# First attention layer of a four-layer stack on one core: the projection as pairs of half-row chunks, with its groups moved into the last pair and the output projection

## The reference

```python
def swa_sink_attention(h, w_qkv, q_gain, k_gain, sinks, w_o):
    qkv = h @ w_qkv                         # 1024 -> 1024 (q) + 256 (k) + 256 (v)
    q = rmsnorm(q, q_gain); k = rmsnorm(k, k_gain)   # per head of 64
    # 4 key/value heads, 4 query heads for each; a query sees the last 128 keys
    scores = q @ k / 8 - slope * dist, masked
    p = softmax([scores, sink])[..., :-1]
    return (p @ v) @ w_o                    # 1024 -> 1024
```

## Time and profile before

| | us |
|---|---|
| median of 3 runs | 1301.46 |
| lowest, highest | 1301.07, 1302.06 |
| span of the profiled execution (first to last instruction) | 1299.9 |
| TensorE matmul busy in it | 1265.0 (97%) |
| VectorE, ScalarE, GpSimd busy | 900.1, 697.7, 139.2 |
| chain that ended last: TensorE, VectorE, ScalarE | 81%, 11%, 4% |

### The profile page before, as it was taken

The page is one execution under the profiler, slowest core; times in us unless marked ns, Lnnn a source line. Parts: engine busy times, 40 slices in busy tenths (PEclk is TensorE's granted clock), DMA queues, the critical chain, the costliest instruction groups (busy, mean ns, idle before and its releaser), DMA issues.

```text
span 1299.9 us, 19368 instructions
## 1 busy us (share of the span) xinstructions
PE 1265.0 (97%) x7906; PEld 1125.9 (87%) x7906; DVE 900.1 (69%) x1151; ACT 697.7 (54%) x894; POOL 139.2 (11%) x168
## 2 busy tenths in 40 slices
PE   9999999999899999999999999999999999899997
PEld 8888888889688888889888888889999999888886
DVE  6876655667866666567877666588898885865556
ACT  5445555456655455444844444448876763444441
POOL 0000000005604000010000000000325342000000
PEclk9999999999799999999999999999999999999999
DMA  8675766644158766666146555554544335465551
GB/s 276 200 232 159 215 194 194 195 162 163 34 146 211 215 187 188 190 182 213 42 163 226 189 188 189 186 168 151 154 139 142 127 117 169 162 208 188 189 193 64
DMA packets 214888, 224.52 MB, mean 173 GB/s; under 512 B 7312, under 2 KB 192016, under 8 KB 214672
## 3 DMA queue, kind: packets, MB, share of 16 engines
q1 hardware_dynamic: 211472, 213.41, 51.5%
q10 hardware_dynamic: 2304, 7.77, 1.7%
q0 software_dynamic: 1024, 2.10, 1.0%
HBM read 222.20 MB, written 1.05 MB: 172 GB/s over the span
## 4 chain that ended last, share of the span: by engine, by line
PE 81%; DVE 11%; ACT 4%; issue 2%; POOL 2%; DMA 1%; DVEq 0%; SPq 0%; ACTq 0%
PE ps L509 20%; PE ps L733 19%; PE ps L500 12%; PE ps L520 7%; PE ps L530 5%; DVE wlo L1607 3%; PE ps L1028 3%; PE ps L694 2%; ACT whi L1143 2%; PE ps L481 2%; PE ps L483 2%; PE ps L482 2%; PE ps L492 1%; DVE ssm_taps L2055 1%; PE ps L599 1%
## 5 line engine op out<-in xcount | busy, mean ns | idle before, releaser
L1607 DVE TENSOR_TENSOR wlo<-raw,whi 128x2048 fp32r<-128x2048 f32 x202 | 462.9, 2300 | 143.2 <-ACT whi L1143 142.5
L1143 ACT ACTIVATE whi<-raw 128x2048 fp32r<-128x2048 f32 x202 | 384.4, 1908 | 58.3 <-PE ps L733 29.7
L509 PE MATMUL ps<-act,whi 128*128 128x512 f32 x1264 | 300.3, 390 | 0.0
L509 PEld LDWEIGHTS ps<-act,whi 128*128 128x128 f32 x1264 | 235.0, 188 | 47.2
L500 PEld LDWEIGHTS ps<-act,wlo 128*128 128x128 f32 x1416 | 181.0, 191 | 8.0 <-DVE wlo L1607 1.8
L500 PE MATMUL ps<-act,wlo 128*128 128x256 f32 x1416 | 184.0, 283 | 1.2 <-DVE wlo L1607 1.2
L1190 ACT ACTIVATE low_sb<-ps 128x512 f32<-128x512 f32 x88 | 52.4, 595 | 186.4 <-PE ps L500 186.4
L520 PE MATMUL ps<-whi,act 128*128 128x256 f32 x736 | 136.0, 285 | 1.3 <-DVE act L1688 1.3
L520 PEld LDWEIGHTS ps<-whi,act 128*128 128x128 f32 x736 | 115.2, 191 | 2.7 <-DVE act L1688 1.3
L733 PE MATMUL ps<-whi,hidhi 128*128 128x512 f32 x368 | 114.1, 391 | 1.2 <-DVE hidlo L1812 1.2
L733 PE MATMUL ps<-wlo,hidhi 128*128 128x512 f32 x368 | 113.7, 390 | 0.0
(11 more groups left out here) (236 smaller groups left out, 1748.0 us busy)
## 6 DMA issues: line engine op xcount, KB each, us to landing
raw<-in_mlp_w SPq DMA_DIRECT2D x128, 512.0 KB, 4.4
raw<-in_ffn_w_gate_up SPq DMA_DIRECT2D x88, 512.0 KB, 5.2
raw<-in_ssm_w_in SPq DMA_DIRECT2D x50, 512.0 KB, 4.8
raw<-in_ffn_w_down SPq DMA_DIRECT2D x44, 512.0 KB, 5.0
raw<-in_conv_w_in SPq DMA_DIRECT2D x24, 512.0 KB, 4.7
raw<-in_attn_w_in SPq DMA_DIRECT2D x18, 512.0 KB, 4.8
raw<-in_ssm_w_out SPq DMA_DIRECT2D x16, 512.0 KB, 4.1
raw<-in_attn_w_qkv SPq DMA_DIRECT2D x12, 512.0 KB, 4.4
```

Of the source, the lines that this page charges most:

```text
L509: e.matmul(bank2(b + f), hi[:, k, f * P:(f + 1) * P], act[:, :, k, :], start=k == 0, stop=False, skip_group_check=True)
L1143: e.activation(whi[s][:, :], raw[s][:, :], ACT.Copy).then_inc(*rounded.up(c))
L1607: e.tensor_tensor(wlo[s][:, :], raw[s][:, :], f32(whi[s][:, :]), ALU.subtract).then_inc(*split.up(c))
```

## The change

The projection is cut into three pairs of `half_rows` chunks of 512 columns: keys and values, queries 0 to 511, queries 512 to 1023. Each pair gives one bank for each token tile, with 512-wide matmuls. Copies, squares, sums, rates, norms and transposes now go by pair `p` and token tile `m`. Groups are ordered `m = n // 2 % 2, g = 2 * (n // 4) + n % 2`: groups 0 and 1 are the first token tile, 2 and 3 the second, with the first eight heads; 4 to 7 the same with the last eight. All groups use one pair of score banks (2 and 3) and one bank for `mix` (6), so `score(n)` waits for `biased(n - 1)` and `mix(n)` for `out_lo(n - 1)`. Groups 0 to 3 stand between the products of the last pair. Groups 4 to 7 stand between those of the output projection, whose chunks now come as upper rows of both column halves, then lower rows. The four output tiles end in banks 0, 1, 7 and 2. VectorE adds `x` only in `next_stage`, after `lo(FFN1)`. A second factor of 1.0 stands in `make_bias`.

The diff, cut to its core:

```diff
         def swa_group(n):
-            m, g = divmod(n, 4)
+            m, g = n // 2 % 2, 2 * (n // 4) + n % 2
...
+        PAIR_COLS = (D, 0, 512)
+        PAIR_BANKS = ((0, 1), (2, 3), (0, 1))
+        PROJECTED = {(0, 0): 0, (1, 0): 1, (0, 1): 7, (1, 1): 2}
...
-            for n in range(QKV1 // WIDE):
-                columns(SWA + n, A["attn_w_qkv"][0], QKV_COLS["swa"][n])
-            for n in range(4):
-                half_rows(SWA + 6 + n, A["attn_w_o"][0], n)
+            for p in range(3):
+                for half in range(2):
+                    half_rows(swa_pair(p, half), A["attn_w_qkv"][0], half, PAIR_COLS[p])
+            for half in range(2):
+                for col in range(2):
+                    half_rows(swa_out(half, col), A["attn_w_o"][0], half, 512 * col)
...
# TensorE, swa()
+                take(0)
+                e.wait_ge(*split(swa_pair(0, 0)))
+                e.wait_ge(*act_lo(2, 0, 0))
+                rows(0, 0, 0)
+                e.wait_ge(*rounded(swa_pair(0, 1)))
+                e.wait_ge(*act_lo(2, 0, 1))
+                for j in range(2):
+                    rows(0, 1, 0, (2 * j, 2 * j + 1), (0, 2))
+                    turn_tile(2, 1, (j,))
+                e.wait_ge(*split(swa_pair(0, 1)))
+                rows(0, 1, 0, passes=(1,)).then_inc(*tile_made.up("swa", 0, 0))
...
+                e.wait_ge(*split(swa_pair(2, 0)))
+                rows(2, 0, 0, (0, 1))
+                heads(1, 0, 6)
+                rows(2, 0, 0, (2, 3))
+                score("swa", 0)
+                e.wait_ge(*split(swa_pair(2, 1)))
+                rows(2, 1, 0).then_inc(*tile_made.up("swa", 2, 0))
+                heads(1, 1, 7)
+                score("swa", 1)
+                e.wait_ge(*copied("swa", 0, 1))
+                rows(2, 0, 1, (0, 1))
+                turn_probs("swa", 0)
+                score("swa", 2)
+                rows(2, 0, 1, (2, 3)).then_inc(*multiplied.up(swa_pair(2, 0)))
+                mix("swa", 0)
+                turn_probs("swa", 1)
+                score("swa", 3)
+                rows(2, 1, 1, (0, 1))
+                mix("swa", 1)
+                heads(2, 0, 7)
+                turn_probs("swa", 2)
+                score("swa", 4)
+                rows(2, 1, 1, (2, 3)).then_inc(*multiplied.up(swa_pair(2, 1)))
+                mix("swa", 2)
+                turn_probs("swa", 3)
+                score("swa", 5)
...
+                out_rows(0, 0, 0)
+                mix("swa", 3)
+                e.wait_ge(*qk_lo("swa", 2, 0))
+                heads(2, 1, 7)
+                turn_probs("swa", 4)
+                score("swa", 6)
...
+                out_rows(1, 0, 0).then_inc(*part.up("swa", 0, 0))
+                mix("swa", 7)
+                e.wait_ge(*split(swa_out(1, 1)))
+                out_rows(1, 1, 0).then_inc(*part.up("swa", 0, 1))
+                e.wait_ge(*out_lo("swa", 6))
+                out_rows(1, 0, 1, (0, 1))
+                e.wait_ge(*out_lo("swa", 7))
+                out_rows(1, 0, 1, (2, 3)).then_inc(*multiplied.up(swa_out(1, 0)))
+                for k in range(4):
+                    last = out_rows(1, 1, 1, (k,))
+                    if k in (1, 2):
+                        turn_tile(3, 0, (k - 1,))
+                last.then_inc(*multiplied.up(swa_out(1, 1)))
                 free.clear()
-                project("swa", SWA + 6, 3, lambda p: out_lo("swa", 4 + p), True)
+                free[0], free[1], free[2] = added("swa", 0, 0), added("swa", 1, 0), added("swa", 1, 1)
...
# ScalarE, swa()
+                exps(2)
+                mix(0)
+                turn(1)
+                hi(swa_out(0, 0))
+                heads(2, 0, 7)
+                exps(3)
+                mix(1)
+                turn(2)
+                copy(2, 1)
+                square_heads(2, 1)
+                exps(4)
...
+                turn(7)
+                mix(7)
                 e.wait_ge(*biased("swa", N_GROUPS - 1))
                 load_rows(3, A["norm_ffn"][1])
-                project("swa", c0 + 6, 3)
+                hi(FFN1)
+                next_stage(3, "swa", FFN1 + 1, (0, 1))
...
# VectorE, swa()
+                weigh(1)
+                heads(1, 1, 7)
+                normalise(0)
+                head_sum(2, 0)
+                weigh(2)
+                normalise(1)
+                rest(0)
+                head_norm(2, 0)
+                weigh(3)
+                normalise(2)
+                rest(1)
+                heads(2, 0, 7)
+                lo(swa_out(0, 0))
+                weigh(4)
+                head_sum(2, 1)
+                normalise(3)
...
+                lo(FFN1)
+                next_stage(3, FFN1 + 1, sum_tile)
...
# GpSimd
             make_bias(0)
-            head_rate(0)
+            head_rate(0, 0)
+            head_rate(0, 1)
             make_bias(1)
-            for n in range(1, 5):
-                head_rate(n)
-            for n in range(2, N_GROUPS):
+            head_rate(1, 0)
+            head_rate(1, 1)
+            make_bias(2)
+            head_rate(2, 0)
+            make_bias(3)
+            make_bias(4)
+            head_rate(2, 1)
+            for n in range(5, N_GROUPS):
                 make_bias(n)
```

440 lines of the change are left out of this document (260 added, 180 removed).

## The result

| | before | changed |
|---|---|---|
| median of 4 runs each, us | 1301.76 | 1313.44 |
| lowest, highest | 1301.07, 1302.40 | 1312.94, 1314.31 |
| ratio, 95% interval | 1 | 1.0091 [1.0079, 1.0102] |
| span of the profiled execution | 1299.9 | 1311.3 |
| TensorE, VectorE, ScalarE, GpSimd busy | 1265.0, 900.1, 697.7, 139.2 | 1267.7, 899.6, 697.7, 128.8 |

The forecast was 1309.7 us within 1302.3 to 1315.8: the sign and the range held, and the time came out 3.7 us above the number. The loss lies in the touched layer: the changed trace is 0.25 us late ahead of it (its first product starts at 290.85 instead of 290.60), and the first transpose of token tile 1 for the next FFN stands at 400.27 instead of 389.33, +10.9 us of the span's +11.4. That transpose marks the end of the layer in what follows.

A forecast was written before the change was run, and what follows sets the result against it. TensorE, busy 97% of the span, was taken as the bound. Terms 3.1 + 1.6 - 1.8 + 0.5 + 2.0 + 2.0 + 0.9 = +8.3 us raised the span to 1308.2, hence a median of 1309.7 us, range 1302.3 to 1315.8.

The forecast's parts named there:

- Wait at the start, +3.1: Layer start: TensorE runs out of products and waits 3.8 us for VectorE's low part of chunk 50, costing 3.1 us.
- Half clock behind it, +1.6: After the wait at the layer's start, TensorE runs at half clock and loses 1.6 us, ends 0 and 1.9.
- Wide matmuls, -1.8: Projection: 144 matmuls of 512 columns replace 288 of 256, taking 32.8 us instead of 34.6, a gain of 1.8 us.
- The groups' waits, +0.5: Attention groups: TensorE's waits for VectorE plus shape changes lose 12.5 us where 12.0 were lost before, +0.5 us.
- Clock in the groups, +2.0: Attention groups: long waits bring half clock in three pieces of 3.7 us, costing 2.0 us, ends 0 and 5.
- scores 3 to 5 six to seven microseconds apart: Sign in the groups' trace that would show the forecast right: successive scores 3 to 5 spaced by that much.
- The reserve of 12.0 us: Attention stretch before the change: 6.5 us idle plus at most 5.5 us lost to half clock could be won.
- End, +2.0: Layer's end: additions of token tile 0 queue behind chunk 59's low part, 8.8 us against 6.8 of products, +2.0 us.
- into the FFN, +0.9: Passage to the FFN: the next transpose comes 5.1 us after the last product instead of 4.2, +0.9 us.
- GpSimd: Bias tiles and roots on GpSimd: the extra factor of 1.0 priced at nothing, every bias ready in time.
- the rival at 0.15: Group 5's bias waits for VectorE low parts, and the clock costs its upper 5 us: +14.3, 1315.8 us; chance 0.15.
- The groups overlap as drawn: Rival in the groups: losses fall to 3 us and the clock term to 0, giving 1298.3 us; chance 0.13.

The follow-up runs named there:

- experiment 1: Changed kernel with TensorE's products at the layer's start reordered, so twelve stand in the wait for chunk 50's low part: 1307.92 us, ratio 1.0045 to before.
- experiment 6: Changed kernel with each 512-wide product of the projection's pairs split into two of 256 columns, for timing only: 1312.90 us, ratio 1.0084 to before.
- experiment 3: Changed kernel with 59 products of zeros added in six of TensorE's waits of the groups: 1307.85 us, ratio 1.0048 to before.
- experiment 9: Kernel before the change with 47 products of zeros added between its groups' steps: 1302.45 us, ratio 1.0006 to before.
- experiment 2: Changed kernel with VectorE's sums and scales at the layer's end put ahead of low parts of the FFN's first weights: 1312.39 us, ratio 1.0074 to before.
- experiment 4: Changed kernel with GpSimd making group 5's bias ahead of the power of head tile (2,1): 1312.65 us, ratio 1.0083 to before.
- experiment 12: Changed kernel with the orders of experiments 1, 2, 4 and 5, plus earlier normalisations and head tiles, later low parts: 1297.82 us, ratio 0.9971 to before.
- experiment 5: Changed kernel with VectorE normalising group 3 ahead of the sum of squares of head tile (2,1): 1311.39 us, ratio 1.0078 to before.

## Why the prediction was right

- **Wait at the start, +3.1.** Right: 3.61 us of wait; experiment 1 takes away 3.1 by putting twelve products into it.
- **Half clock behind it, +1.6.** Nearly right: the eight products from 300.57 to 303.82 take 3.25 us instead of 8 x 0.228 = 1.8, so 1.4 are lost; experiment 1 gets 1.2 back. The two terms made 4.7 us, and score 0 gained 3.9.
- **Wide matmuls, -1.8.** On TensorE 1.0 of the 1.3 us due before score 0 (experiment 6), but only some 0.5 of all of it is left at the end of the layer. The gap that the Trainium skill gives ("TensorE: Matmul & The Clock Gate", "Back-to-back issue gap") would make an estimated 0.4 us of all 144 products; the trace does not agree, with 1.0 us on TensorE before score 0 alone.
- **The groups' waits, +0.5.** I had 11.7 us of waits; the trace has 9.6, both with score 0's. The places were right (turns 0 to 3, scores 4 and 6). The turns of groups 2 and 3 were 1.0 and 0.8 too dear, group 5's 0.6, and score 4 was 0.7 too cheap.
- **Clock in the groups, +2.0.** This is the step that failed in size. The prediction took "three pieces of 3.7 us" at "at most 1.8 each", part of it hidden. There were two, of 6.4 and 6.9 us, with 12.4 us of work in them, so up to 6.2 us lost, of which experiment 3 shows 4.8 on the path. The length was taken from the shorter piece of before; and the work that the change puts behind the wait, twelve wide products in a row, was not looked at. For the same reason the sign "scores 3 to 5 six to seven microseconds apart" did not hold: they are 8.0 and 9.0 us apart.
- **The reserve of 12.0 us.** "Up to 12.0 us could be won there" counted 5.5 us of lower clock in the kernel before, all of it as lost. In experiment 9 the full clock brings 1.9 us up to group 2's turn, and from there VectorE's chain takes up what is left. So not all of the 5.5 us stood on the path, and taking the sum against before by "lost now 12.0, then 12.5" came out too low; by how much is not shown.
- **End, +2.0, and into the FFN, +0.9.** The mechanism was right, the size too dear. There is a wait of 1.44 us for `h` ahead of token tile 0's transposes where before had none, and one of 1.36 for `x`; the wait of 0.95 us that before had ahead of the next transpose is 0.17 now. That transpose comes 4.8 us after the last product against 4.2 before, +0.6. Experiment 2 gets 1.6 us back from both.
- **GpSimd.** Priced at nothing; the rival at 0.15 had a late bias of group 5 as its mechanism. The wait came (1.37 us), but experiment 4 shows that it costs nothing that can be measured. Its dear clock did come, but by group 3's wait for VectorE.
- **The groups overlap as drawn** (0.13): not with VectorE's order as written; with the order of experiment 12 they do.

So the sign came for the reasons given, and the nearness of the number is in part luck: the start, the waits and the end were 0.8, 2.1 and 0.9 us too dear, the clock in the groups 2.8 us too cheap, and the gain of the wide products 1.3 us too large.

By the traces, the start's order, the filled waits and the end's order give back 3.9 + 4.8 + 1.6 = 10.3 of the span's 11.4 us; 0.7 of these lie outside the layer (0.25 ahead of it, 0.5 behind). What is left is the balance of longer waits in the groups against wide products, which no run takes apart.

## What to carry to other kernels

An interleaving on one engine is only as good as the order of the queues that feed it. Here four queues' orders, with no work changed, were worth 15.6 us, more than the change cost. Behind each wait, look at what is queued on the engine waited for: an instruction that is itself idle there (the head sum, 2.34 us), or work wanted only later (the low parts), goes behind the one that is wanted first.

Price a drop of the clock by the work that stands behind the wait, not by its length alone. A cheap test is to fill the waits with products of zeros: if the time falls, the clock is on the path. If it doesn't, look in the trace whether the products themselves hold anything up before another engine's chain is named: in experiment 9 they stood ahead of a score that waited for nothing and took 1.4 us.

## What the runs showed of the hardware

The bias tiles on GpSimd became cheaper when a second multiplication by 1.0 was added to the instruction. The median tile is 404 ns against 847, in the same 32 instructions:

```profile
L2498 POOL TENSOR_SCALAR bias<-table x32: 297/404/2231, 295.7 to 360.6; 128x128 f32<-128x128 f32 x16, 128x256 f32<-128x256 f32 x16
```

The clearest pair is group 0's four tiles, of one shape and in the same place of both kernels, behind the same wait:

```profile
295.46 2.30 POOL L2315 TENSOR_SCALAR bias<-table 128x128 f32<-128x128 f32 x4 [1.36 <-DVE h L1663]
```
```profile
295.71 1.38 POOL L2498 TENSOR_SCALAR bias<-table 128x128 f32<-128x128 f32 x4 [1.35 <-DVE h L1810]
```

I had priced the factor at nothing, and this is nearly all of the 10.4 us by which GpSimd's busy time fell (139.2 to 128.8): in the stretch 290 to 370 us the tiles' line went from 25.9 to 15.1 us. No run takes the factor away by itself, and why it helps was not tried. The longest tile is as long as before.

The piece at half clock behind one and the same wait of 3.61 us is not of one length: with the same instructions around it, it ended at about 303.4 us in the changed kernel's profile, near 305.8 in that of experiment 2 and near 306.7 in that of experiment 5. That alone moves score 0 by about 1.5 us, and it is as large as several of the effects tested here.
